# A decoder trunk's first attention: the diagonal of row maxima made by ScalarE in four scaled copies, not by one VectorE product

## The reference

```python
q = _rmsnorm(proj[..., :hw].reshape(bsz, seq, FOX_HEADS, HEAD_DIM), g_q)
k = _rmsnorm(proj[..., hw:2 * hw].reshape(bsz, seq, FOX_HEADS, HEAD_DIM), g_k)
c = jnp.cumsum(log_f, axis=1).transpose(0, 2, 1)
for blk in range(seq // Q_BLOCK):                     # blocks of 128 queries
    s = einsum(q[:, t0:t1], k[:, :t1]) * scale
    s = s + c[:, :, t0:t1, None] - c[:, :, None, :t1]  # causal mask follows
    p = jax.nn.softmax(s, axis=-1)
    outs.append(einsum(p, v[:, :t1]))
```

## Time and profile before

| | |
|---|---|
| median of 3 runs | 1234.91 us (1232.08 to 1237.37) |
| profiled execution | 1231.83 us, its span 1230.0 us |
| TensorE matmul busy | 1185.0 us, 96% |
| VectorE, ScalarE, GpSimd busy | 576.5, 480.2 and 559.3 us |
| mean granted TensorE clock | 0.991 |
| first attention (pairs' projections to the last product with V) | about 73 to 276 us of the span |

### The profile page before, as it was taken

One profiled execution on the slowest core, in us unless ns is written; L12 is line 12 of the kernel. 1 busy time (PEld: TensorE's weight loads), 2 busy tenths in 40 slices (PEclk: granted clock), 3 DMA queues, 4 the chain that ended last, 5 costly groups with the idle time before them and its releaser, 6 DMA issues.

```text
span 1230.0 us, 15042 instructions
## 1 busy us (share of the span) xinstructions
PE 1185.0 (96%) x5634; PEld 985.2 (80%) x5634; DVE 576.5 (47%) x717; ACT 480.2 (39%) x594; POOL 559.3 (45%) x383
## 2 busy tenths in 40 slices
PE   6999999989999999999999799989999999999998
PEld 6887888877888888888888588877888888888887
DVE  5857878866633100234223778986643200233100
ACT  5348778854322211122224555653422111222121
POOL 4512533524566544565445602224565544555542
PEclk9999999989999999999999899999999999999999
DMA  6221121122233344223332201112233322333331
GB/s 223 84 69 35 35 68 34 34 69 69 69 103 102 103 135 138 79 92 103 103 102 74 97 1 35 35 35 57 80 103 102 103 84 87 103 102 102 98 109 34
DMA packets 142236, 101.20 MB, mean 82 GB/s; under 512 B 3128, under 2 KB 141552, under 8 KB 142192
## 3 DMA queue, kind: packets, MB, share of 16 engines
q1 hardware_dynamic: 142128, 100.56, 27.7%
q10 hardware_dynamic: 64, 0.03, 0.0%
HBM read 98.47 MB, written 2.12 MB: 82 GB/s over the span
## 4 chain that ended last, share of the span: by engine, by line
PE 67%; issue 15%; DVE 8%; POOL 6%; ACT 3%; DMA 1%; SPq 0%; POOLq 0%; ACTq 0%; DVEq 0%
PE ps L1221 21%; PE ps L1222 21%; PE ps L1223 21%; POOL w_lo L412 5%; POOL fox_sq_lo L419 1%; DVE xn_lo L864 1%; DVE rst L836 1%; DVE swa_diag L1167 1%; DVE x_hat L857 1%; ACT w_hi L471 1%; DMA x_in<-in_x 1%; ACT q_hl L733 0%; DVE q_hl L1124 0%; DVE sqt L840 0%; PE ps L1543 0%
## 5 line engine op out<-in xcount | busy, mean ns | idle before, releaser
L412 POOL TENSOR_TENSOR w_lo<-stage,w_hi 128x512 fp32r<-128x512 f32 x356 | 520.5, 1492 | 476.8 <-ACT w_hi L471 470.1
L471 ACT ACTIVATE w_hi<-stage 128x2048 fp32r<-128x2048 f32 x88 | 168.4, 1914 | 476.3 <-PE ps L1223 471.4
L1221 PE MATMUL ps<-xn_hi,w_hi 128*128 128x512 f32 x720 | 285.8, 397 | 0.4 <-issue 0.3
L1222 PE MATMUL ps<-xn_lo,w_hi 128*128 128x512 f32 x720 | 280.9, 390 | 0.0
L1223 PE MATMUL ps<-xn_hi,w_lo 128*128 128x512 f32 x720 | 280.8, 390 | 0.0
L1221 PE MATMUL ps<-r_hi,w_hi 128*128 128x512 f32 x512 | 199.8, 390 | 0.0
L1223 PE MATMUL ps<-r_hi,w_lo 128*128 128x512 f32 x512 | 199.3, 389 | 0.0
L1222 PE MATMUL ps<-r_lo,w_hi 128*128 128x512 f32 x512 | 199.2, 389 | 0.0
L1221 PEld LDWEIGHTS ps<-xn_hi,w_hi 128*128 128x128 f32 x720 | 135.7, 188 | 31.3 <-issue 3.1
L1222 PEld LDWEIGHTS ps<-xn_lo,w_hi 128*128 128x128 f32 x720 | 135.6, 188 | 29.1 <-issue 1.9
L1223 PEld LDWEIGHTS ps<-xn_hi,w_lo 128*128 128x128 f32 x720 | 135.5, 188 | 28.6
(11 more groups left out here) (207 smaller groups left out, 1623.9 us busy)
## 6 DMA issues: line engine op xcount, KB each, us to landing
stage<-in_w_up SPq DMA_DIRECT2D x32, 1024.0 KB, 5.4
stage<-in_w_down SPq DMA_DIRECT2D x32, 1024.0 KB, 5.5
stage<-in_w_in_a SPq DMA_DIRECT2D x16, 512.0 KB, 5.1
stage<-in_w_in_a SPq DMA_DIRECT2D x4, 1024.0 KB, 6.3
stage<-in_w_out_a SPq DMA_DIRECT2D x4, 1024.0 KB, 5.0
stage<-in_w_q_b SPq DMA_DIRECT2D x4, 1024.0 KB, 5.0
stage<-in_w_out_b SPq DMA_DIRECT2D x4, 1024.0 KB, 5.0
x_in<-in_x SPq DMA_DIRECT2D x4, 512.0 KB, 7.5
```

The source lines that it names most:

```text
L412: ins = nc.gpsimd.tensor_tensor(w_lo[:, s, c], stage[:, s, c], w_hi[:, s, c].bitcast(F32), ALU.subtract)
L471: nc.scalar.activation(w_hi[:, s, :], stage[:, s, :], ACT.Copy).then_inc(w_hi_ready, 1)
L1221: mm(out_, st_hi, mv_hi, start=start, stop=False)
L1222: mm(out_, st_hi, mv_lo, start=False, stop=False)
```

## The change

Three edits. VectorE's product is removed, and with it its waits. ScalarE makes the same `diag` with four `Identity` activations of 128 columns for each half, the scale being the column of `nm`; it waits for the maxima of the half, and for the transposed scores of the pair before, which read the old `diag`. These eight activations stand after the split and ahead of `fox_rstd(i, 0)` in steps 1 to 7 (in step 1 after `fox_cross(0)` too), and for pair 7 ahead of its exponentials. Last, the two sums of squares of pair 0 are issued at k = 2 of the projection that they stand in, not at k = 4.

```diff
+            def fox_diag(j):
+                for e in range(2):
+                    act.wait_ge(fox_max_ready, 2 * j + e + 1)
+                    after(act, fox_scores_done, 2 * j - 1 + e)
+                    for qb in range(TB):
+                        ins = nc.scalar.activation(diag[:, e, qb * P:(qb + 1) * P], ident, ACT.Identity,
+                                                   scale=nm[:, e, qb:qb + 1])
+                    ins.then_inc(fox_diag_ready, 1)
+
             def fox_step(i, landed_count, s):
                 fox_square(i, 0)
                 split(landed_count, U_PAIR + i + 1, s)
                 if isinstance(i, int) and i == 1:
                     fox_cross(0)
+                fox_diag(i - 1)
                 fox_rstd(i, 0)
...
+            fox_diag(7)
             fox_exp(7, 0)
...
                     ins.then_inc(fox_max_ready, 1)
-                    dve.wait_ge(fox_max_ready, 2 * j + e + 1)
-                    after(dve, fox_scores_done, 2 * j - 1 + e)
-                    V.tensor_tensor(diag[:, e, :].rearrange("p (b n) -> p b n", b=TB),
-                                    ident[:, None, :].to_broadcast([P, TB, P]),
-                                    nm[:, e, :, None].to_broadcast([P, TB, P]), ALU.mult).then_inc(fox_diag_ready, 1)
...
-                    if k == 4 and sum_before is not None:
+                    if sum_before is not None and k == (2 if isinstance(sum_before[0], int) and sum_before[0] == 0 else 4):
                         fox_sum(*sum_before)
```

## The result

The changed kernel takes 1236.99 us (median of 20 runs, 1234.78 to 1241.3) against 1234.11 us (20 runs, 1231.92 to 1237.37): ratio 1.0024, interval 1.0015 to 1.0034. It is 2.9 us slower, a little under half of the forecast's 5.8 us, and on its side. The profiled execution took 1234.78 us, its span 1233.0.

What follows compares the result with a forecast made beforehand. TensorE, busy 96% of the span, was taken to bound the kernel, so only chains it waits for count. Terms -0.9 + 0.25 + 2.8 + 2.4 + 1.7 - 0.45 = +5.8 us on 1233.5 gave 1239.3 us, range 1231 to 1246.

Steps and rivals of the forecast that it cites:

- The place in the queue: ScalarE's in-order queue: eight copies ahead of fox_rstd start it 2.4 us later; the 22.4 us off VectorE is worth nothing by length.
- The copy: One diagonal on ScalarE: 0.40 us per 128-column scaled copy, 1.28 us for four, ends 0.84 and 1.60.
- Step 1: Early sums of pair 0 gain up to 3.1 us, but ScalarE's queue leaves 0.9: sum at 108.6 instead of 109.50.
- Steps 2 to 6: Late squares delay TensorE's sum: +0.25 us in step 2, 0.7 us in each of steps 3 to 6, +2.8 us.
- Step 7 and its clock: Five oa_hi copies leave ScalarE no slack: squares +2.4 us, TensorE idle 2.8 us, low clock behind it +1.7 us.
- The tail: Pair 7's diagonals ready earlier, -0.45 us; wait stays 2.5 us with the low clock behind it; bounds 0 and -0.45 - 3.05.
- the first rival: Late squares hidden in steps 2 to 6 because w_lo gets faster, no low clock in step 7: +1.0, 1234.5 us; chance 0.20.
- the clearly slower one: New idle times of steps 1 and 7 both bring low clock, copies cost 1.60 us: +12, 1245.5 us; chance 0.12.
- The faster one: Both low-clock stretches vanish and the copies fit ScalarE's idle slots: -6.6, 1226.9 us; chance 0.07.

Runs made afterwards that it cites:

- dummy_copies: Kernel before, VectorE still making the diagonals, plus eight ScalarE copies a step into an unread tile: 1247.92 us against 1234.99, ratio 1.0094.
- one_half: Changed kernel, but in steps 1 to 7 ScalarE copies only half 0 and VectorE makes half 1: 1230.36 us against 1234.33, ratio 0.9968.
- diag_only: Changed kernel with pair 0's two sums of squares back at k = 4: 1237.10 us against 1234.99 for the kernel before, ratio 1.0016.
- oa_spread: Changed kernel with three of step 7's five oa_hi copies made in step 6: 1233.82 us against 1234.99 for the kernel before, ratio 0.9983.
- tail_only: Kernel before with only pair 7's two diagonals made by ScalarE, ahead of its exponentials: 1233.13 us against 1234.33, ratio 0.9990.
- k2_only: Kernel before with only pair 0's two sums of squares moved to k = 2, VectorE still making diagonals: 1232.43 us against 1234.99, ratio 0.9978.

## Why the prediction was right, and where it was off

- **The place in the queue: shown.** I said that what counts is `fox_rstd` behind eight copies and the second half's maxima, not the 22.4 us taken off VectorE. Waits for the squares in all seven steps and dummy_copies (+11.6 us) say the same, and with half of the copies (one_half) the waits of steps 2 to 6 are gone. `fox_rstd` starts 2.2 us later in step 3, with 2.4 forecast.
- **The copy: 0.391 us in 64, and 1.28 us for four, as worked out from the earlier trace rows.** The group by shape of ScalarE in the changed kernel:

```profile
L618 ACT ACTIVATE diag<-kept,nm 128x128 fp32r<-128x128 f32 x64 | 20.4, 391 | 4.0 <-DVE nm L1001 3.6
```

- **Step 1: shown.** Forecast 108.6 for the sum and "whatever the clock does ahead of it"; measured 108.49, and 14.73 and 14.75 us with either clock.
- **Steps 2 to 6: mis-sized.** Forecast +0.25 and 4 x 0.7, measured -0.08 and 4 x 0.45. The long form of `fox_sq_lo` was right (1.83 against 1.74 us), but I let ScalarE's instructions follow each other without overlap at two seams: `fox_rstd` after the copies, `raw` after it. In the trace `fox_rstd` starts 0.09 us before the copies end (148.33 + 1.28 against 149.52), `raw` 0.09 us before `sqt` does. And the eight reductions in a row took 3.27 us, where I had 3.38, so half 1's copies began 0.13 us sooner.
- **Step 7 and its clock: right.** +2.4 forecast, +2.23 measured; a wait of 2.8 against 2.64 us; and the low clock behind it, 1.7 us. In diag_only, with a wait of 2.65 us, it came too; in oa_spread, with 0.86 us, it did not.
- **The tail: the step that failed.** "The wait stays 2.5 us, so I leave the low clock behind it." The wait did stay (2.56 us), and the clock was still 1.00 in the profile and in five of seven with ScalarE's copies. The 3.05 us lay inside my bounds but not in the sum. On average the gain is smaller: tail_only has 1.2 us (0.1 to 2.2), of which 0.4 is the wait.
- **The balance.** At pair 7's scores the changed kernel is 4.20 us late; 0.8 us of clock in the tail, by tail_only's median, makes 3.4. Before also has steps of 23.3 us in some executions (two more in k2_only's and tail_only's profiles than in before's), which would take up to 0.9 off. That is 2.5 to 3.4 us against 2.9 measured. How often each stretch of low clock occurs per execution was not measured, so this split is worked out, not shown.
- **A row misread.** I took the 0.69 us product (238.83) for one "where GpSimd is quiet". It is not: `w_lo` starts 0.08 us after it and takes longer than in step 3, 6.43 us against 5.94.

```profile
238.91 6.43 POOL L412 TENSOR_TENSOR w_lo<-stage,w_hi 128x512 fp32r<-128x512 f32 x4 [0.64 <-ACT w_hi L471]
```

  So the two rows differ in which of the two started first, not in a busy and a quiet GpSimd. The sum didn't use the row, but the first rival leaned on it. TensorE's waits by my own four figures add up to 8.1 us, not 7.9.
- **Luck in the number.** The time fell into the range, but +2.9 us lies nearer to the first rival's +1.0 than to my +5.8. It is the waits in steps 2 to 7, not the time, that decide for the forecast; steps mis-sized by 1.3 us in sum and a tail that gave back what I had left out brought the time down together.

Of the rivals, the clearly slower one needed the low clock in step 1 too: TensorE waited 1.55 us there and it did not come. The faster one had the right idea of both old low-clock stretches vanishing, and failed where it was said to, at slots too short for the copies. The first rival had `w_lo` right (1538 to 1346 ns a piece) and not what follows: GpSimd, freed, stood waiting for ScalarE.

## What to carry over

Before moving work to an engine with idle time, look at where in its queue it will stand and what it waits for: eight short copies behind a late wait delayed everything issued after them, while four behind an early wait fitted a slot and were free in the steady steps. Splitting the work so that each engine makes the half whose input comes at its own idle time (half 0 to ScalarE while VectorE reduces half 1) undid the move's loss, 0.9968 against 1.0024. Most of its gain over the kernel before comes from the edits beside it: with those and VectorE's diagonals the ratio is 0.9973. A combination has to be compared with the best kernel that lacks only the part in question. And a unit of time saved just ahead of a dense stretch of matmuls may be worth more or less than itself, by the clock behind it.

## What was not expected of the hardware

- TensorE's clock fell to 1.2 GHz some 2 us after a wait of only 1.22 us (k2_only, 0.51 from 98.0 to 101.5 us), while in the changed kernel the same wait had 1.00 behind it; at 2.55 us it fell in two profiles of seven, at 2.58 us in four of four. One profile can't tell whether a change removes such a stretch.
- GpSimd's `w_lo` got faster by 12.5% (1538 to 1346 ns) without a change to it, because VectorE's product no longer ran beside it.
- The steady step of the kernel before has two lengths, 22.8 and 23.3 us, with the same code, and the start order of two instructions goes with it. In its steps 3 to 6 `w_lo` starts 0.01 to 0.04 us before VectorE's product of half 0, the product takes 1.80 to 1.83 us and `w_lo` 5.93 to 5.95. In step 2 the product starts 0.08 us before `w_lo` (124.47, 124.55) and takes 0.69, and `w_lo` takes 6.41; in k2_only the long steps 4 and 6 have 0.69 and 6.48 to 6.50. TensorE then waits 0.39 to 0.47 us for the squares behind `w_lo`. So a few hundredths of a microsecond go with a step 0.5 us longer. Where the two start within 0.01 us both outcomes occur (dummy_copies, step 4: 0.69 and 6.04), so there the trace doesn't tell which was first.
